# Attention and pool output weights fetched four tiles per load instead of two

## What is computed

```python
def _token_mixing(u, w_in, ..., w_attn_o, w_pool_o, w_out, cos, sin):
    z = u @ w_in
    q, k, v, p, g_a, g_p = jnp.split(z, [i1, i2, i3, i4, i5], axis=-1)
    ...
    y_attn = _window_attention(q, k, v, sinks) @ w_attn_o      # (512, 512) @ (512, 1024)
    y_pool = _multiscale_pool(p, w_pool_grp, pool_scale) @ w_pool_o   # (512, 512) @ (512, 1024)
    merged = jax.nn.sigmoid(g_a) * y_attn + jax.nn.sigmoid(g_p) * y_pool
    return merged @ w_out                                      # (512, 1024) @ (1024, 1024)
```

## Time and profile before

| what | value |
|---|---|
| runs | 2158.65, 2163.26, 2165.34 us |
| median | 2163.26 us |
| span of the profiled execution | 2167.4 us |
| TensorE matmul busy | 2103.8 us, 97% |
| GpSimd busy | 955.2 us, 44% |
| VectorE busy | 987.4 us, 46% |
| ScalarE busy | 571.0 us, 26% |
| weight stream (q1) | 264.8 MB, 40.8% of 16 DMA engines' span |

### The profile page before, as it was taken

One profiled execution on the slowest core, in us unless ns is written; L12 is line 12 of the kernel. 1 busy time (PEld: TensorE's weight loads), 2 busy tenths in 40 slices (PEclk: granted clock), 3 DMA queues, 4 the chain that ended last, 5 costly groups with the idle time before them and its releaser, 6 DMA issues.

```text
span 2167.4 us, 30219 instructions
## 1 busy us (share of the span) xinstructions
PE 2103.8 (97%) x10214; PEld 1775.1 (82%) x10214; DVE 987.4 (46%) x1609; ACT 571.0 (26%) x850; POOL 955.2 (44%) x471
## 2 busy tenths in 40 slices
PE   7999999998999999999999999999989999999999
PEld 7888888886887888878888888888868788888887
DVE  5733234268658643223345422335856766332332
ACT  1322222231422422222222222222233224123222
POOL 0644344345245554334445533444443456443443
PEclk6999999999999999999999999999999999999999
DMA  7344345332345355254425524442423544432333
GB/s 272 108 136 140 91 146 163 71 117 83 93 127 183 88 162 161 68 146 137 136 59 172 155 75 145 137 134 67 141 69 112 156 151 126 131 100 79 98 100 104
DMA packets 343634, 267.49 MB, mean 123 GB/s; under 512 B 27094, under 2 KB 306990, under 8 KB 343470
## 3 DMA queue, kind: packets, MB, share of 16 engines
q1 hardware_dynamic: 341792, 264.80, 40.8%
q10 hardware_dynamic: 1678, 0.55, 0.1%
HBM read 263.21 MB, written 2.10 MB: 122 GB/s over the span
## 4 chain that ended last, share of the span: by engine, by line
PE 79%; issue 12%; POOL 5%; DVE 2%; DMA 1%; ACTq 0%; DVEq 0%; POOLq 0%; ACT 0%; SPq 0%
PE bank L1214 23%; PE bank L1215 22%; PE bank L1216 22%; POOL w_lo L561 5%; PE bank L1277 1%; PE bank L1278 1%; PE bank L1281 1%; PE ps L1485 1%; PE ps L1299 1%; POOL pool_s L575 1%; PE ps L1237 1%; PE ps L1236 1%; PE ps L1235 1%; PE bank L1235 1%; PE bank L1237 1%
## 5 line engine op out<-in xcount | busy, mean ns | idle before, releaser
L561 POOL TENSOR_TENSOR w_lo<-stage,w_hi 128x1024 fp32r<-128x1024 f32 (+2 forms) x342 | 856.8, 2519 | 1107.2 <-ACT w_hi L619 1060.2
L1214 PE MATMUL bank<-u_hi,w_hi 128*128 128x512 f32 x1792 | 713.2, 398 | 10.5 <-issue 7.5
L1215 PE MATMUL bank<-u_lo,w_hi 128*128 128x512 f32 x1792 | 701.4, 391 | 0.0
L1216 PE MATMUL bank<-u_hi,w_lo 128*128 128x512 f32 x1792 | 701.3, 391 | 0.0
L619 ACT ACTIVATE w_hi<-stage 128x1024 fp32r<-128x1024 f32 (+2 forms) x340 | 353.5, 1071 | 207.2 <-DMA stage<-in_w_pool_o 66.3
L1214 PEld LDWEIGHTS bank<-u_hi,w_hi 128*128 128x128 f32 x1792 | 339.2, 189 | 82.9 <-issue 11.8
L1216 PEld LDWEIGHTS bank<-u_hi,w_lo 128*128 128x128 f32 x1792 | 338.9, 189 | 72.0
L1215 PEld LDWEIGHTS bank<-u_lo,w_hi 128*128 128x128 f32 x1792 | 339.4, 189 | 70.9 <-issue 2.9
L1214 PE MATMUL bank<-h_hi,w_hi 128*128 128x512 f32 x744 | 292.1, 393 | 6.1 <-POOL w_lo L561 6.1
L909 DVE TENSOR_TENSOR prod<-silu,bank 128x512 f32<-128x512 f32 x88 | 60.5, 687 | 515.9 <-PE bank L1216 493.1
L889 DVE SCALAR_TENSOR_TENSOR ada_acc<-ada_stage,c_act,ada_acc 128x512 f32<-128x512 f32 x252 | 268.0, 1064 | 52.5 <-DMA ada_stage<-in_w_ada 47.9
(11 more groups left out here) (160 smaller groups left out, 1680.6 us busy)
## 6 DMA issues: line engine op xcount, KB each, us to landing
stage<-in_w_ff_up SPq DMA_DIRECT2D x176, 512.0 KB
ada_stage<-in_w_ada SPq DMA_DIRECT2D x256, 256.0 KB, 3.5
stage<-in_w_ff_down SPq DMA_DIRECT2D x32, 1408.0 KB
stage<-in_w_in SPq DMA_DIRECT2D x18, 1024.0 KB
stage<-in_w_out SPq DMA_DIRECT2D x10, 1024.0 KB
ada_first<-in_w_ada SPq DMA_DIRECT2D x16, 512.0 KB, 12.2
stage<-in_w_in SPq DMA_DIRECT2D x16, 256.0 KB
stage<-in_w_in SPq DMA_DIRECT2D x8, 512.0 KB
```

The source lines that it names most:

```text
L561: nc.gpsimd.tensor_tensor(stage_tile(w_lo, kind, n), t, hi_tile(n, depth(kind, n)), ALU.subtract).then_inc(lo_ready, 1)
L1214: mm(bank[n % BANKS][:, :], hi[:, k, :], rhs_hi(k), start=(k == 0), stop=False)
L1215: mm(bank[n % BANKS][:, :], hi[:, k, :], rhs_lo(k), start=False, stop=False)
L1216: last = mm(bank[n % BANKS][:, :], lo[:, k, :], rhs_hi(k), start=False, stop=(k == k_n - 1))
```

## The change

The first 12 of the 16 y tiles come in three loads of four tiles (1 MB) in place of six of two. The layout in the slot is 512 columns wide: attention columns of two tiles side by side, then pool columns of two tiles side by side, so that a contiguous run is 256 floats (1 KB). Tiles 38 to 41 stay as two loads of two. `stage_tile` finds a tile in the wide layout. The mixer has 24 loads in place of 27, and the y stage 15 weight DMAs in place of 24; from tile 38 on each load has the same slot as before.

```diff
 MIX_LOADS = ([(t, 2) for t in range(0, T_GA, 2)]
              + [(T_GA + 5 * j + t, k) for j in range(3) for t, k in ((0, 1), (1, 2), (3, 2))] + [(T_Y - 1, 1)]
-             + [(t, 2) for t in range(T_Y, MIX_TILES, 2)])
+             + [(t, 4) for t in range(T_Y, T_Y + 12, 4)] + [(t, 2) for t in range(T_Y + 12, MIX_TILES, 2)])
@@ def stage_tile(t, kind, n):
             k = depth(kind, n)
+            if kind == "mix" and T_Y <= n < T_Y + 12:
+
+                part = 2 * (j % 2) + j // 2
+                return t[s][:, 0:k * 4 * P].rearrange("p (k c) -> p k c", c=4 * P)[:, :, part * P:(part + 1) * P]
             return t[s][:, 0:k * 2 * P].rearrange("p (k c) -> p k c", c=2 * P)[:, :, j * P:(j + 1) * P]
@@ def mix(l):   (SyncE)
+                    elif k == 4:
+                        m = (t - T_Y) // 2
+                        wide = stage[s][:, 0:QPK * 4 * P].rearrange("p (k c) -> p k c", c=4 * P)
+                        for g in range(N_KV):
+                            sp.dma_start(wide[g * HEAD:(g + 1) * HEAD, :, 0:2 * P],
+                                         ao_v[l, g, :, :, m * P:(m + 2) * P]).then_inc(loaded[s], LOADED // 4)
+                        sp.dma_start(wide[:, :, 2 * P:4 * P], po_v[l, :, :, m * P:(m + 2) * P]
+                                     ).then_inc(loaded[s], LOADED // 2)
                     elif t < T_OUT:
```

## The result

The changed kernel is slower: 2181.89 us median of 4 runs (2178.33 to 2192.52), against 2162.82 us for the kernel before, measured beside it in 4 runs. The ratio is 1.0097, 95% interval 1.0068 to 1.0127, or about 19 us. Predicted were 2154.7 us, range 2150.0 to 2162.5, with a chance of 0.05 on this side. The prediction was wrong in sign.

What follows compares the result with a forecast made beforehand. TensorE was taken as the bound, losing time in the y stage to late weights behind SP's queue. Terms -5.3 - 4.7 + 1.4 = -8.6 us took the median from 2163.26 to 2154.7 us, range 2150.0 to 2162.5.

Steps and rivals of the forecast that it cites:

- What bounds the kernel now: Y stage, reductions behind tiles 28 to 38: TensorE loses 5.3 and 4.7 us to weights late through SP's queue.
- Tile 34's load and tile 38's load: Y stage: both loads come earlier, so waits before these tiles and the lower clock go, -5.3 and -4.7 us by layer.
- Fewer and longer runs: Wide weight loads: 1 KB runs at 346 GB/s take 3.0 us in place of 4.2, all off the path.
- Runs of 512 bytes are as fast: Rival, chance 0.10: wide loads at 250 GB/s delay pieces, PE waits 0.9 us behind tile 28 per layer; 2156.5 us.
- Pieces behind a bigger load: Pieces 28 and 29 land up to 0.9 us later, hidden before the reduction behind tile 28; nothing in the sum.
- if it has, the pieces are later than I think: Sign to check: idle time before the reduction behind tile 28, where none was expected, would mean later pieces.
- the cover of 1.2 us: Reduction behind tile 28: piece 31 is finished at 641.0, the reduction began at 642.18, so 0.9 us delay is hidden.
- I see nothing in the change that moves this pair relative to PE: Loads of tiles 40 and 42: lateness of 1.4 us stays in layer 1 and appears in layer 0, +1.4 us.
- The spare of 0.9 us: Tile 40, layer 1: weights usable at 1728.5, PE began the tile at 1729.4, so no wait was expected.
- the wait moves on: Rival, chance 0.20: tile 40 or 42 comes 2 us later, costing 4.7 us in each layer; 2161.3 us.
- The start of tile 42: Forecast 1.4 us late in both layers, with ScalarE waiting for the w_out DMA.
- Slower: Rival, chance 0.06: wide loads delay pieces, pieces hold VectorE, tile 40's load comes 9 us later; +9.0, 2172.3 us.

Runs made afterwards that it cites:

- experiment 10: Kernel before, two-tile loads kept, with pieces 28 and 29 ahead of tile 28's load and one piece less ahead of loads from tile 32 to 40: 2154.62 us.
- experiment 1: Changed kernel with conditioning pieces 28 and 29 put ahead of the load of tiles 30 to 33 in SP's queue: 2163.6 us, ratio 1.0013 to the kernel before.
- experiment 5: Changed kernel with the wide load's columns side by side in the slot, without gaps between runs: 2173.28 us, ratio 1.005 to the kernel before.
- the repeat: The changed kernel measured once more, unedited, beside the follow-up kernels: 2178.28 us, ratio 1.0094 to the kernel before.
- experiment 7: Changed kernel where ScalarE rounds tiles 30 to 33 two tiles later, spreading GpSimd's subtractions: 2168.83 us, ratio 1.0053 to the kernel before.
- experiment 9: Changed kernel where ScalarE rounds tile 44 only once VectorE has merged the last pair: 2173.94 us, ratio 1.0053 to the kernel before.

## Why the prediction was wrong

**What bounds the kernel now: right.** The 5.3 and 4.7 us were late weights behind SP's queue; experiment 10 removes them by nothing but the queue's order, and both stretches fall to 28.10 us, where the prediction had 28.05.

**Tile 34's load and tile 38's load: right**, and so is the "-5.3 and -4.7 us" in experiment 1 (28.10 us for 33.35 and 32.75). In the change itself only 2.1 and 1.5 us of it arrived, since the stretch now ran behind a new wait, at a lower clock. (The tiles were placed wrongly in the text, "tiles 30 and 31 now come with tile 28's load": tiles 28 and 29 come with tile 26's, and 30 to 33 stand where tile 28's load stood. The times of tile 34's load do not hang on it.)

**"Fewer and longer runs": the size failed.** I took 346 GB/s at full share from the earlier trace rows, a w_out load, for all 1 KB runs, and had 3.0 us for a wide load. The load of tiles 30 to 33 moved 222 GB/s at a share of 1.06 in layer 0 and 252 at 0.95 in layer 1. So the row of w_out was not the nearest one, and no gain over the 250 of the 512-byte runs is left. Why w_out's loads are faster stays open: the gaps between the runs in the slot do not explain it, since with the runs side by side the load moved 305 and 234 GB/s (experiment 5). The rate in the rival "Runs of 512 bytes are as fast", 250 GB/s, was nearer, and its wait behind tile 28 was there, only larger (0.9 us for 3.5).

**"Pieces behind a bigger load": the step that failed first.** "They land up to 0.9 us later" was 2.3 us later. And the cover of 1.2 us was read as time in which nothing else changes: but that VectorE would "use pieces 30 and 31 as much later" left out that the same load lets GpSimd run on through five tiles, and that VectorE's work beside it takes 8.9 us in place of 6.5. Term in the sum: 0. Measured: a wait of 3.5 us in each layer (2.7 in one layer of the repeat) and 3.1 of lower clock behind it, 6.7 us a layer. Two experiments that leave the load's size and layout as they are take the wait away: the order of the queue (experiment 1) wholly, GpSimd's pauses (experiment 7) for the most part. I had named the test ("if it has, the pieces are later than I think") and gave the rival with this place 1.8 us for both layers.

**"I see nothing in the change that moves this pair relative to PE": the second step that failed.** What moved is PE. Tile 40's load in the kernel before, layer 0, and in experiment 1:

```profile
668.95 1.41 SPq L505 DMA_DIRECT2D stage<-in_w_attn_o  x2
```

```profile
662.25 1.39 SPq L517 DMA_DIRECT2D stage<-in_w_attn_o  x2
```

Counted from the reduction behind tile 28, it is issued after 26.8 us in layer 0 of the kernel before and 28.7 in layer 1, and after 27.1 and 27.3 us in experiment 1: no later. But PE reaches the reduction behind tile 38 after 28.1 us, where it came after 33.35 and 32.75. The spare of 0.9 us was read from layer 1 "with PE running undisturbed since tile 34"; but there PE had stood 2.62 us before tile 34, and VectorE had caught up so far that it waited for PE:

```profile
1717.77 0.69 DVE L1043 SCALAR_TENSOR_TENSOR merge<-gate_p,bank 128x512 f32<-128x512 f32 x1 [0.66 <-PE bank L1216]
```

The spare belonged to the disturbed kernel. In the change the load is issued after 30.5 us in both layers, since VectorE had itself stood behind the first wait. It also waited for piece 37, which now stands behind the load of tiles 38 and 39:

```profile
662.33 1.88 DVE L901 SCALAR_TENSOR_TENSOR ada_acc<-ada_stage,c_act,ada_acc 128x512 f32<-128x512 f32 x1 [1.44 <-DMA ada_stage<-in_w_ada]
```

Piece 40 needs piece 38 used, and tile 40's load stands behind piece 40. How much that new order of load and pieces adds was not measured by itself. The rival "the wait moves on" had this place right and its price low: 4.7 us a layer, with the time of "-10.0 + 9.4 - 1.4" (2161.3 us; experiment 1, where this place is what is left, took 2163.6). Against undisturbed, the last stretch of the change is 6.2 and 9.7 us longer, tile 42's waits included; before it was 0.6 and 1.2.

**The start of tile 42.** Forecast was 1.4 us late in both layers for the w_out DMA. It was 0.98 us late in layer 0 and not late in layer 1, and a wait that I had not named stood inside the tile: `u_lo` of the last pair, 0.91 and 2.12 us, which is GpSimd's burst again (experiment 9).

**"Slower" came true, by more than its place.** Its mechanism, late pieces that hold VectorE and through it tile 40's load, was at work, but I argued it away by adding only transfer times ("three loads of 0.9 us each cannot add up to 4.5"). The loss is the first wait, which I had at 0, and the tile 40 wait together.

**What stays open.** Why the two layers trade places in the last stretch (42.77 and 46.28, 46.36 and 41.72) was not found. The share of the transfer's rate in the 2.3 us was not separated from the mere size of the load: experiment 5 and the repeat overlap. Nor was it found why the first wait is 3.5 us in one run and 2.7 in another.

## What to carry over

When a load on an in-order DMA queue grows, look at what stands behind it and at who is waiting for that, before what it saves; here the same gain was to be had by order alone. Spare time read next to an existing wait is not there once that wait is removed: ask what had caught up during it. And weights that arrive in bigger lots let GpSimd run in bursts, which here slowed VectorE beside it.

## What the runs showed of the hardware

- Wide loads with 1 KB runs into a slot with gaps moved 222 GB/s at a share of 1.06 in layer 0 and 252 at 0.95 in layer 1; with the runs side by side it was 305 and 234 at the same time after the issue. 512-byte runs came to 250, scaled up from a share of 0.52. The gaps made no difference that holds in both layers, and a gain from runs of 1 KB over 512 bytes is not shown.
- VectorE's 128x512 cast took 0.43 us alone and 2.53 us beside GpSimd's unbroken subtractions, and the subtraction 0.69 and 2.76.
- A wait of 3.5 us on TensorE cost 3.1 us more in the stretch behind it, with a granted clock of 0.57 over the first 8 us. A wait of 2.7 us cost 1.7 (experiment 5, layer 1) to 3.0 us (repeat, layer 1).
